# Two-layer block on one core: 128x128 value matmuls, a rounded causal mask, a second bank for the early columns, and the MLA high parts moved to VectorE

## The reference, cut to what matters

```
s = q @ k.T * scale            # fox heads: plus F[t] - F[s], the cumulative log forget gates
s = where(causal mask, s, -1e30)
p = softmax(s)
o = p @ v                      # 16 heads, 64 value columns each
mix = concat(o_mla, o_fox) @ w_out
```

## Time and profile before

| what | value |
|---|---|
| runs (3) | median 1349.61 us, 1349.4 to 1350.0 |
| profiled execution, span | 1348.6 us; the page gives no other time of it |
| TensorE matmul / weight load busy | 98% / 96% |
| VectorE, ScalarE, GpSimd busy | 72%, 55%, 26% |
| granted TensorE clock, mean | 0.996 |
| first `scores` of step 4 | 104.32 us from the span's start |
| first matmul of attn_out | 161.32 us |

### The profile page before, as it was taken

The page is one execution under the profiler, slowest core; times in us unless marked ns, Lnnn a source line. Parts: engine busy times, 40 slices in busy tenths (PEclk is TensorE's granted clock), DMA queues, the critical chain, the costliest instruction groups (busy, mean ns, idle before and its releaser), DMA issues. The chain is left out here.

```text
span 1348.6 us, 28895 instructions
## 1 busy us (share of the span) xinstructions
PE 1323.8 (98%) x10822; PEld 1289.3 (96%) x10822; DVE 966.7 (72%) x1454; ACT 746.7 (55%) x1214; POOL 357.0 (26%) x377
## 2 busy tenths in 40 slices
PE   9999999999999999999999999999999989999997
PEld 8886699999999999999999999999999989999997
DVE  5867687655587777655665569998559897999844
ACT  5555654444444454444545557666457886766642
POOL 3522023310011243200546313333102101433310
PEclk9999999999999999999999999999999999999998
DMA  9430055555555455555535545554564545555451
GB/s 303 169 114 1 32 178 198 187 188 187 187 180 178 173 176 183 195 181 180 209 126 175 193 164 188 187 187 141 208 213 156 174 167 192 189 186 187 150 202 54
DMA packets 35372, 230.53 MB, mean 171 GB/s; under 512 B 4062, under 2 KB 5214, under 8 KB 11910
## 3 DMA queue, kind: packets, MB, share of 16 engines
q1 hardware_dynamic: 34228, 226.99, 47.9%
q10 hardware_dynamic: 1058, 2.38, 0.5%
HBM read 228.17 MB, written 1.05 MB: 170 GB/s over the span
## 5 line engine op out<-in xcount | busy, mean ns | idle before, releaser
L381 DVE TENSOR_TENSOR wlo<-raw,whi 128x1024 fp32r<-128x1024 f32 (+1 forms) x446 | 526.0, 1182 | 91.0 <-ACT whi L375 88.3
L416 PE MATMUL ps<-xhi,whi 128*128 128x256 f32 (+2 forms) x2048 | 579.7, 283 | 4.0 <-DVE wlo L381 2.8
L417 PE MATMUL ps<-xlo,whi 128*128 128x256 f32 (+2 forms) x2048 | 577.9, 282 | 0.0
L418 PE MATMUL ps<-xhi,wlo 128*128 128x256 f32 (+2 forms) x2048 | 576.7, 282 | 0.0
L375 ACT ACTIVATE whi<-raw 128x1024 fp32r<-128x1024 f32 (+2 forms) x444 | 447.1, 1010 | 147.3 <-PE ps L418 137.2
L416 PEld LDWEIGHTS ps<-xhi,whi 128*128 128x128 f32 x2048 | 386.5, 189 | 9.0 <-issue 4.6
L418 PEld LDWEIGHTS ps<-xhi,wlo 128*128 128x128 f32 x2048 | 387.2, 189 | 0.0
L417 PEld LDWEIGHTS ps<-xlo,whi 128*128 128x128 f32 x2048 | 384.7, 188 | 0.3
L416 PE MATMUL ps<-hhi,whi 128*128 128x256 f32 (+1 forms) x1184 | 334.3, 282 | 4.4 <-DVE hlo L1687 3.5
L418 PE MATMUL ps<-hhi,wlo 128*128 128x256 f32 (+1 forms) x1184 | 333.2, 281 | 0.0
L417 PE MATMUL ps<-hlo,whi 128*128 128x256 f32 (+1 forms) x1184 | 333.0, 281 | 0.0
(11 more groups left out here) (298 smaller groups left out, 1276.4 us busy)
## 6 DMA issues: line engine op xcount, KB each, us to landing
raw<-w SPq DMA_DIRECT2D x182, 1024.0 KB, 4.9
raw<-w SPq DMA_DIRECT2D x40, 768.0 KB, 4.1
raw<-w SPq DMA_DIRECT2D x4, 512.0 KB, 5.6
h<-x_fm ACTq DMA_DIRECT2D x4, 272.0 KB, 5.5
out_fm<-h SPq DMA_DIRECT2D x8, 128.0 KB, 2.0
ws<-ws_src ACTq DMA_DIRECT2D x1, 512.0 KB, 3.6
bs<-bs_rows ACTq DMA_DIRECT2D x1, 512.0 KB, 6.3
consts<-constants SPq DMA_DIRECT2D x1, 508.0 KB, 10.1
```

The lines of the kernel that those rows point to most:

```text
L381: nc.vector.tensor_tensor(wlo[:, w, 0:n], raw[:, slot, col:col + n], whi[:, w, 0:n].bitcast(F32), ALU.subtract).then_inc(wlo_done, 3 if fr ...
L416: nc.tensor.matmul(o, hi, xh, start=start, stop=False)
L417: nc.tensor.matmul(o, hi, xl, start=False, stop=False)
L418: mm = nc.tensor.matmul(o, lo, xh, start=False, stop=stop)
```

## The change

- `values`: the padded rows of the early keys are cleared, in `v_tok` (rows 16 to 127 of the first tile) and in `prob_0`, so that L1155 runs with 128 rows. The three products take the 128 value columns of a pair of heads and write all 128 rows of the bank; the reader still takes the 64 rows of its own head.
- `scores`: identity and mask are copied once, rounded to fp32r, to `mask_r`, and the mask is added by one fp32r matmul.
- `turn`: from item 8 on the early columns alternate between banks 7 and 6, and the wait is for the item before the last one.
- `high` of h8 to h15 moves from ScalarE (step st-3) to VectorE, just ahead of `low` (step st-4); the halo copies of h8 to h15 move from ScalarE to GpSimd.
- GpSimd gets two memsets (1024 and 516 columns), one rounding copy (256 columns) and eight halo copies.

```diff
@@ buffers
+            mask_r = part("mask_r", [P, 2 * P], F32R)
-        prob_0 = [flat_x[0:META, x * T1:(x + 1) * T1] for x in range(2)]
+        prob_0 = [flat_x[:, x * T1:(x + 1) * T1] for x in range(2)]
@@ TensorE, scores
+                if j == 1:
+                    pe.wait_ge(s("mask_rounded"), 1)
-                    mm = nc.tensor.matmul(ps[:, b, z - P:z], ident, mask, start=False, stop=True)
+                    mm = nc.tensor.matmul(ps[:, b, z - P:z], mask_r[:, 0:P], mask_r[:, P:2 * P], start=False, stop=True)
@@ TensorE, turn
+                turn_bank = 6
                 if j == 0:
                     pe.wait_ge(vt_done, 6)
+                elif j <= LAST_SHARED:
+                    pe.wait_ge(pt0_done, j)
                 else:
-                    pe.wait_ge(pt0_done, j)
+                    turn_bank = 6 + (j - LAST_SHARED) % 2
+                    pe.wait_ge(pt0_done, j - 1)
+                    pe.wait_ge(k_out, 2 * HEADS)
@@ TensorE, values
-                if i == HEADS:
-                    pe.wait_ge(d_done, HEADS + 1)
-                o = ps[64 * (hd % 2):64 * (hd % 2) + DV, b, 0:T1]
-                v = slice(hd * DV, (hd + 1) * DV)
-                nc.tensor.matmul(o, v_tok[0:META, w, 0, v], pt0, start=True, stop=False)
+                pe.wait_ge(d_done, i + 1)
+                if i == 0:
+                    pe.wait_ge(s("prob_0_set"), 1)
+                o = ps[:, b, 0:T1]
+                v = slice(hd // 2 * P, (hd // 2 + 1) * P)
+                nc.tensor.matmul(o, v_tok[:, w, 0, v], pt0, start=True, stop=False)
@@ VectorE
+            def high(i):
+                w, hd = heads[i][3:5]
+                rows = HALF[hd % 2]
+                dve.wait_ge(pv_done, i + 1)
+                nc.vector.tensor_copy(chi[rows, 4 * (1 - w) + hd // 2, C1:T0],
+                                      ps[rows, 4 + i % 2, 0:T1]).then_inc(ohi_done, 1)
...
                 if st >= 4 and items[st - 4][0] == "h":
+                    if items[st - 4][1] >= HEADS:
+                        high(items[st - 4][1])
                     low(items[st - 4][1])
@@ ScalarE
-                        act.wait_ge(sel_done, 1)
+                        act.wait_ge(s("v_meta_set"), 1)
...
-                    if i == 1:
-                        halo(HEADS)
-                if i != HEADS:
+                if i < HEADS:
                     halo(i)
-                if st >= 3 and items[st - 3][0] == "h":
+                if st >= 3 and items[st - 3][0] == "h" and items[st - 3][1] < HEADS:
                     high(items[st - 3][1])
@@ GpSimd, after the copy of sel and ahead of mean_eps
+            pool.wait_ge(sel_done, 1)
+            nc.gpsimd.memset(v_tok[:, :, 0, :], 0.0).then_inc(s("v_meta_set"), 1)
@@ GpSimd, after the key rotation
+            pool.wait_ge(consts_in_done, 16)
+            nc.gpsimd.tensor_copy(mask_r[:, :], consts[:, K_IDENT:K_IDENT + 2 * P]).then_inc(s("mask_rounded"), 1)
+            pool.wait_ge(s("mask_rounded"), 1)
+            nc.gpsimd.memset(flat_x[:, 0:2 * T1], 0.0).then_inc(s("prob_0_set"), 1)
+            pool.wait_ge(s("prob_0_set"), 1)
@@ GpSimd, after the query statistics, ahead of attn_out's sums
+            pool.wait_ge(pt0_done, D1 + 1)
+            for i in range(HEADS, NHD):
+                hd = heads[i][4]
+                pool.wait_ge(pv_done, i - 1)
+                nc.gpsimd.tensor_copy(prob_0[i % 2][0:META, 0:HALO],
+                                      prob_d[1][:, HALO * hd:HALO * (hd + 1)]).then_inc(d_done, 1)
```

More of the change, by code:

```diff
@@ L806, in program @@
         D1 = items.index(("d", 1))
+        LAST_SHARED = 7
         KEY_SPREAD = {5: 1, 6: 2, 7: 3}
@@ L1129, in turn @@
                 if kind == "d":
-                    nc.tensor.transpose(ps[0:META, 6, 0:META], pr[0:META, 0:META],
+                    nc.tensor.transpose(ps[0:META, turn_bank, 0:META], pr[0:META, 0:META],
                                         ident[0:META, 0:META]).then_inc(pt_ps, 1)
@@ L1136, in turn @@
                 for x, a in enumerate((A, B)):
-                    nc.tensor.transpose(ps[0:META, 6, x * P:(x + 1) * P], pr[:, a:a + META], ident)
+                    nc.tensor.transpose(ps[0:META, turn_bank, x * P:(x + 1) * P], pr[:, a:a + META], ident)
                 for x, a in enumerate((A + META, B + META, B + META + P)):
@@ L1796, in halo @@
                 d = prob_d[i // HEADS][:, HALO * hd:HALO * (hd + 1)]
-                nc.scalar.activation(prob_0[i % 2][:, 0:HALO], d, ACT.Copy).then_inc(d_done, 1)
+                nc.scalar.activation(prob_0[i % 2][0:META, 0:HALO], d, ACT.Copy).then_inc(d_done, 1)
             def turned(j):
@@ L1801, in turned @@
                 act.wait_ge(pt_ps, j + 1)
+                if j == 0:
+                    act.wait_ge(s("prob_0_set"), 1)
+                turn_bank = 6 if j <= LAST_SHARED else 6 + (j - LAST_SHARED) % 2
                 if kind == "d":
-                    nc.scalar.activation(prob_d[i], ps[0:META, 6, 0:META], ACT.Copy).then_inc(pt0_done, 1)
+                    nc.scalar.activation(prob_d[i], ps[0:META, turn_bank, 0:META], ACT.Copy).then_inc(pt0_done, 1)
                     act.wait_ge(pt0_done, j + 1)
-                    if i == 1:
-                        halo(HEADS)
                     return
@@ L1809, in turned @@
                     act.wait_ge(pv_done, i - 1)
-                nc.scalar.activation(prob_0[i % 2][:, HALO:T1], ps[0:META, 6, 0:2 * P], ACT.Copy).then_inc(pt0_done, 1)
+                nc.scalar.activation(prob_0[i % 2][0:META, HALO:T1], ps[0:META, turn_bank, 0:2 * P],
+                                     ACT.Copy).then_inc(pt0_done, 1)
                 if j == 5:
```

## The result

The changed kernel takes 1343.52 us (median of 5, 1342.53 to 1345.00) against 1349.61 for the kernel before (5 runs, 1348.21 to 1351.18); the ratio is 0.9944, with a 95% interval of 0.9921 to 0.9966. By the ratio that is a gain of 7.6 us, by the medians one of 6.1, where 4.0 were forecast: faster, as said, and by more than said.

A forecast was written before the change was run, and what follows sets the result against it. TensorE was taken to set the pace in plain MLA steps, VectorE to hold it back from step 14. Steps 4 to 8 gain 1.4, 9 to 13 0.8, the rest 1.8: 4.0 us, time 1345.6, range 1343.2 to 1348.4.

The forecast's parts named there:

- half-clock stretch: Around 114 to 116 us TensorE ran at 1.2 of 2.4 GHz; such a stretch was said to cost 1.5 us.
- Steps 4 and 5: Heads' stage: TensorE's 0.74 us wait for VectorE's keys in step 5 stays, so together they gain nothing.
- Steps 6 and 7: Heads' stage: VectorE needs 3.73 us per step with the keys, against 4.12 at full clock: 0.39 gained twice.
- The drains: Shape changes of TensorE's operands around the value products: 0.45 us per head, all taken as gone.
- The second bank: Early columns' bank, items above 7: three TensorE waits for bank 6 lifted, 0.6 us of each counted as gain.
- Steps 9 to 13: To about 141.4 us: ScalarE sets the pace until 132, then two heads and one bank wait gain; 0.8 us taken.
- Step 14 to the end: Last 19.9 us before attn_out: VectorE holds TensorE back and needs 18.1 us, a gain of 1.8.
- E: Rival, chance 0.13: VectorE's copy is cheap (last stretch gains 0.5 more) and the half-clock stretch goes (step 6 gains 1.5): 1343.6 us.
- B: Rival, chance 0.16: more idle time on TensorE in the heads' stage brings a second half-clock stretch, costing 1.5 us: 1347.1 us.
- C: Rival, chance 0.05: slower, TensorE at half clock in five of nine steps, VectorE the bound through steps 9 to 17: 1355.1 us.
- A: Rival, chance 0.15: the short fp32r mask costs what the mask did, some 1.1 us less gain: 1346.7 us.
- D: Rival, chance 0.09: 96-row scores or 16-column transposes keep the drains, only masks and banks gain, 1.3 us: 1348.3 us.

The follow-up runs named there:

- third profile before: The kernel before, unchanged, in its third profiled execution, which had no half-clock stretch in the heads' stage: 1349.71 us.
- mask alone: The kernel before with only the mask matmul changed to fp32r, identity and mask rounded once by GpSimd: 1347.46 us, ratio 0.9992.
- changed, narrow values: The changed kernel with the value products back in the old 16x64 and 128x64 operand form: 1347.29 us, ratio 0.9979.
- filled wait: The kernel before with two extra unread fp32 products in step 5, where TensorE idles ahead of the spread of the keys: 1350.39 us, ratio 0.9997.
- second bank alone: The kernel before with only two banks for the early columns of the items above 7: 1348.61 us, ratio 0.9965.

## Why the prediction was right in its sign and short in its size

The stages, without the half-clock stretch: 55.40 before, 49.36 after, a gain of 6.04, against 4.0.

- **Steps 4 and 5, "together gain nothing": the step that failed.** They gained 0.70 + 0.63 = 1.33. It was argued that TensorE waits for VectorE's keys in step 5 and that this stays. A wait stays (0.91 us, ending at 109.03), but its end was taken as fixed, and nothing was counted behind it. The end came 0.85 us earlier, 4.95 us after the start of step 4 instead of 5.80: VectorE's chain began with an idle of 0.83 us in which it waited for TensorE's scores, 0.27 of which the mask took away, and 0.34 + 0.25 more came from instructions that met GpSimd's sums at other moments. Where the late engine had itself been waiting for the early one, its finish moves with the change. And what TensorE does between the keys and the start of step 6, with the value products in it, fell from 3.24 to 2.76 us, by 0.48. The runs with one part alone agree: the mask is worth 0.86 of the 1.33, the values the other 0.47.
- **Steps 6 and 7, 0.39 each.** They gained 0.75 each, all that TensorE could (0.47 + 0.27). Step 6 at full clock takes 4.36, not the 4.12 that the sum took for both, so 0.24 of this was in the base. VectorE's period was right: 3.75 us from peak to peak (112.98 to 116.73) against the 3.73 of the prediction. But a period binds only once the slack is used up. In the third profile before VectorE idled 0.88, 0.64 and 0.28 us ahead of the peaks of steps 6 to 8, and in the changed kernel not at all: the deficit was drawn from that. Step 8, counted at 0.6, gained 0.31 (3.26 to 2.95). Steps 4 to 8 thus gained 20.79 - 17.64 = 3.15 where 1.4 stood in the sum: 1.75 of the 2.0 that were missing.
- **The half-clock stretch** was carried unchanged into the sum. It came in two of four profiles of the kernel before and in none of the changed kernel's: 1.6 us between the two profiled spans, which with 6.04 and the 0.24 by which step 4 started earlier makes the 7.9. No profile shows it as a gain of the change. Among the 12 further runs of the changed kernel and the 25 of the kernel before beside them, those with a mean granted clock of 0.998 have a median span of 1347.65 us before (4 runs) and 1341.95 changed (6 runs), 5.7 apart, near the 6.04. The ratio takes in the other runs, too. Counting kernels with five runs or more, a mean clock of 0.993 or less stands in 14 of 89 runs of the kernel before, in 8 of 24 runs of the two kernels with the fp32r mask and narrow values (mask alone; changed, narrow values), in none of 22 of two more with narrow values (filled wait, second bank alone), and in 1 of 66 runs of the kernels with 128x128 values. So the wide values may spare some stretches at low clock, which would be a gain beyond the 6.04. That is not shown: where in the kernel they lay is known of the profiled runs alone.
- **The drains**, 0.45 per head: 0.47 measured, by the step lengths. The Trainium skill (TensorEngine Tiling (Array Packing), Key Properties) says that changing the tiling mode drains the engine. The trace agrees for both sizes of the value operands, with gaps of 0.17 to 0.39 us; for the 16-column transposes between 128-column products it still shows no gap at 139.94.
- **The mask**, 0.115 saved each: 0.12 between the loads, 0.27 a head, somewhat over the 0.23.
- **The second bank**, 0.6 three times: 0.69 in all in the kernel before, 0.13 in the changed one. `normal` was named as next in line; in the kernel before it was the probabilities' copy on ScalarE (0.72), in the changed kernel both (0.45, then 0.63). This term was oversized by over 1 us.
- **Steps 9 to 13**, 0.8: 0.91, but the size is luck: 0.6 of the working was a bank wait that is worth 0.01 there (13.77 with one bank, 13.76 with two). **Step 14 to the end**, 1.8 by VectorE's 18.1 us: 1.99 and 17.95. This, too, is right in size for a reason that holds in part. VectorE was the bound only from step 17 on, where the step lengths hardly answer to TensorE's work (9.38 us, with narrow values 9.19, with the fp32 mask 9.39) and fall to 8.45 without `high`. Steps 15 and 16 take TensorE's own 2.52. Steps 14 to 16 are alike with `high` on either engine, so there TensorE and, in step 14, the waits for the scaling and for ScalarE's copy set the pace.
- **The move of `high`** costs the change 0.93 us. The sum counted its time on VectorE (0.42 per head) but did not ask what the end of the stage would be without it.
- **VectorE's copy**, 0.42 per head: the rows have 0.41 to 0.43. GpSimd's clearing of v_tok took 0.95, against an estimate of 1.04; rounding and second clearing took 1.27 + 0.53 = 1.80 instead of 0.8. All but 0.16 us were hidden (`early` began at 77.99 against 77.83), and step 4 began no later.
- **The rivals.** E had the time nearly right, 1343.6, for half a reason: the stretch was absent, but the last stretch gained only 0.2 more than forecast. B and C did not come in either profile of the changed kernel, though the kernel before showed what a step at half clock costs: step 7 took 7.22 us instead of 4.12. A and D are refuted by the step lengths.

**What stays open** is what sets off the half clock. It lay in the stage in four of eleven profiles with the fp32 mask and in none of seven with the fp32r mask; it followed waits of 0.72 to 1.22 us in step 5, but waits of 0.73, 0.91 and again 1.22 had none behind them. The fp32r mask does not rule out a low clock either: the mask alone and the changed kernel with narrow values have runs with a mean clock down to 0.990 and 0.980, and no profile tells where these lost it. The Trainium skill (TensorE: Matmul & The Clock Gate, What's actually happening) says that activity holds the clock up and its lack lowers it; these runs neither confirm nor refute it.

## What to carry to other kernels

Ahead of an engine that is said to be late, read what it waited for itself: where that is the engine being relieved, its lateness shrinks with the change. Count also what lies behind the wait, and take into account that idle time ahead of its other work is a reserve that a longer period uses up first. Lifting a wait for a buffer is worth only the distance to the next releaser, so read the end of every other input of the next two instructions before pricing it. Compare stages by step lengths of executions with the same clock, and profile the kernel before more than once when its clock row has a dent.

## What the runs showed of the hardware that was not expected

- A fall to half clock comes and goes between executions of one kernel at nearly the same place: from 113.0 us for 3.4 us, from 112.2 us for 20 us, and not at all, twice. Six of the fourteen profiles without one in the stage show one of some 3.4 us between 1108 and 1117 us.
- 16 rows and 64 columns each put gaps around a product on TensorE, 0.17 in, 0.17 or 0.34 out, and the savings of mending one only (0.13 and 0.08 us) do not add up to that of both (0.47).
- An fp32r product of 128 columns stands 0.12 us ahead of the next load, the same as one of 258 columns: below 258 columns the shorter product brought nothing here.
- On GpSimd a rounding copy of 128x256 took 1.27 us, against 0.53 for clearing 128x516.
